# A decoder layer on one core: the last sums of squares and the scaled output rows are reordered, and the output goes out in six stores

## The reference, cut to what matters

```python
def rms_norm(x, w):
    return x * rsqrt(mean(x * x, axis=-1) + EPS) * w

h = x + rms_norm(mixer(rms_norm(x, n_mix_pre)), n_mix_post)
f = square(relu(rms_norm(h, n_ffn_pre) @ w_up)) @ w_down      # 1024 -> 4096 -> 1024
y = h + rms_norm(f, n_ffn_post)
```

## Time and profile before

| | us |
|---|---|
| median of 3 runs | 1686.3 (1685.75 to 1686.75) |
| profiled execution, its own time | 1687.35 |
| its span, first to last instruction | 1685.5 |
| PE busy | 1568.3 (93%) |
| DVE busy | 929.4 (55%) |
| ACT busy | 508.1 (30%) |
| POOL busy | 714.7 (42%) |
| last instruction of PE's 30 units ends | 1655.1 |
| last DVE instruction ends | 1677.7 |

### The profile page before, as it was taken

How to read it: one execution, slowest core, us unless ns; L and a number is a source line. 1 busy time by engine, 2 the same in 40 slices (tenths; PEclk the granted TensorE clock), 3 DMA queues, 4 the chain that set the end, 5 groups by cost and what they waited for, 6 DMA issues and landing times.

```text
span 1685.5 us, 27881 instructions
## 1 busy us (share of the span) xinstructions
PE 1568.3 (93%) x10984; PEld 1543.1 (92%) x10984; DVE 929.4 (55%) x1186; ACT 508.1 (30%) x693; POOL 714.7 (42%) x512
## 2 busy tenths in 40 slices
PE   5999999999999998999998969999998899999893
PEld 4999999899999997999998869999998899999893
DVE  5898969354473335011425936545556656565756
ACT  4100000322321224000223726544456142423332
POOL 3334434242244123344464634444444444545454
PEclk9999999999999999999999889999999999999997
DMA  5211121123221331111331053444447533324342
GB/s 168 88 49 46 44 64 44 32 76 100 75 94 44 95 103 34 50 44 46 103 109 32 26 198 123 138 149 155 156 140 252 194 126 123 123 92 141 102 137 109
DMA packets 83528, 169.47 MB, mean 101 GB/s; under 512 B 7392, under 2 KB 19424, under 8 KB 81136
## 3 DMA queue, kind: packets, MB, share of 16 engines
q1 hardware_dynamic: 69504, 144.61, 26.1%
q10 hardware_dynamic: 13936, 23.60, 4.3%
HBM read 124.82 MB, written 43.36 MB: 100 GB/s over the span
## 4 chain that ended last, share of the span: by engine, by line
PE 84%; DVE 8%; issue 2%; ACT 2%; DMA 2%; POOL 2%; SPq 0%; ACTq 0%; DVEq 0%; POOLq 0%
PE ps L610 42%; PE ps L952 31%; PE ps L868 3%; DVE tx_l L1845 2%; PE ps L881 2%; DVE fx_l L1845 1%; PE ps L791 1%; PE ps L710 1%; DVE xn_l L1556 1%; PE ps L709 1%; DVE fac L1956 1%; PE ps L636 1%; PE ps L713 1%; POOL w_l L524 1%; PE ps L724 1%
## 5 line engine op out<-in xcount | busy, mean ns | idle before, releaser
L521 POOL TENSOR_TENSOR w_h<-raw,zero 128x512 fp32r<-128x512 f32 x134 | 155.8, 1163 | 540.0 <-PE ps L610 411.6
L952 PE MATMUL ps<-tx_h,w_h 128*128 128x258 f32 x960 | 274.1, 286 | 18.7 <-DVE fac L1954 6.1
L952 PE MATMUL ps<-tx_l,w_h 128*128 128x258 f32 x960 | 273.2, 285 | 0.0
L952 PE MATMUL ps<-tx_h,w_l 128*128 128x258 f32 x960 | 273.2, 285 | 0.0
L579 POOL TENSOR_TENSOR w_l<-raw,w_h 128x512 fp32r<-128x512 f32 x120 | 181.9, 1516 | 183.8 <-ACT w_h L1333 183.7
L610 PE MATMUL ps<-xn_h,w_h 128*128 128x344 f32 x1128 | 248.4, 326 | 5.0 <-DVE xn_l L1556 4.0
L610 PE MATMUL ps<-xn_l,w_h 128*128 128x344 f32 x1128 | 242.0, 321 | 0.0
L610 PE MATMUL ps<-xn_h,w_l 128*128 128x344 f32 x1128 | 241.2, 320 | 0.0
L952 PE MATMUL ps<-fx_h,w_h 128*128 128x258 f32 x720 | 209.3, 291 | 28.7 <-DVE fac L2002 15.1
L952 PE MATMUL ps<-fx_l,w_h 128*128 128x258 f32 x720 | 207.1, 288 | 0.0
L952 PE MATMUL ps<-fx_h,w_l 128*128 128x258 f32 x720 | 207.0, 288 | 0.0
(11 more groups left out here) (269 smaller groups left out, 2629.4 us busy)
## 6 DMA issues: line engine op xcount, KB each, us to landing
raw<-wseq_dram SPq DMA_DIRECT2D x264, 256.0 KB, 2.7
hq_g<-hidden_scratch SPq DMA_DIRECT2D x14, 1032.0 KB, 8.1
hidden_scratch<-hq_g SPq DMA_DIRECT2D x8, 1032.0 KB, 5.9
stg_a<-hidden_scratch SPq DMA_DIRECT2D x7, 1032.0 KB, 6.7
stg_b<-hidden_scratch SPq DMA_DIRECT2D x7, 1032.0 KB, 6.4
hidden_scratch<-stg_b SPq DMA_DIRECT2D x6, 1032.0 KB, 5.8
rope<-rope_dram ACTq DMA_DIRECT2D x2, 2064.0 KB, 8.1
h_res<-xT_dram ACTq DMA_DIRECT2D x1, 4128.0 KB, 14.1
```

The costliest lines, as they stand in the source:

```text
L521: pool.tensor_tensor(hi, raw[:, s, :], zero[:, 0:1].broadcast_to([P, SLOT]), ALU.add).then_inc(w_hi, 1)
L952: out = pe.matmul(ps[:, 2 * n + s, 0:HC], RINGS[q % RING][wa][:, kk * P:(kk + 1) * P], OPS[x][xb][:, QK * kh + kk, at_:at_ + HC], start=(i ...
```

## The change

The squares: DVE's folds are written by a helper `fold(squares, row, shift, n)`. In the last unit all seven rows 0 to 6 of t = 0 are folded into row 0 by the end of step 3, in five folds instead of two; PE takes the first half's sum ahead of step 6, as ones on row 0 and ones on row 3 (8 PE instructions where 4 stood, in front of the step instead of in its middle). ACT runs `f_rms(0, 3)` directly behind the square of row 7 of t = 1, ahead of `down_gain(7, HALVES[1])`, e7 and the square of row 6.

The output rows: `out_norm` writes one scaled row into a PSUM pair (3, a or c) instead of into `fac`, and `out_residual` adds the residual from there into `fac`, one row per instruction. The rows of both halves are interleaved, so that an addition mostly follows its product by one other instruction. The addition e7 and `root_argument(1, b)` stand among the rows of the first half.

The stores: rows 0 to 2, 3 and 4, and 5 to 7 of each half leave as three stores; for t = 1 the one of rows 3 and 4 is last.

```diff
--- before.py
+++ after.py
@@ -493,12 +493,18 @@
 sp.dma_start(stg_a[:, 0:QK, 0:HT], hscr[:, KHALVES[0], HALVES[1]]).then_inc(h_ld[1], 16)
 sp.dma_start(stg_b[:, 0:QK, 0:HT], hscr[:, KHALVES[1], HALVES[1]]).then_inc(h_ld[1], 16)
 for t in range(2):
-    sp.wait_ge(y_dve, t + 1)
-    sp.dma_start(yT[:, 0:YD, HALVES[t]], fac[:, 0:YD, HALVES[t]]).then_inc(y_st, 16)
+    sp.wait_ge(y_dve, YD * t + 3)
+    sp.dma_start(yT[:, 0:3, HALVES[t]], fac[:, 0:3, HALVES[t]]).then_inc(y_st, 16)
+    if t == 0:
+        sp.wait_ge(y_dve, YD)
+        sp.dma_start(yT[:, 3:YD, HALVES[t]], fac[:, 3:YD, HALVES[t]]).then_inc(y_st, 16)
     sp.wait_ge(y_pool, t + 1)
     sp.dma_start(yT[:, YD:8, HALVES[t]], fac[:, YD:8, HALVES[t]]).then_inc(y_st, 16)
-
-sp.wait_ge(y_st, 16 * 4)
+    if t == 1:
+        sp.wait_ge(y_dve, 2 * YD)
+        sp.dma_start(yT[:, 3:YD, HALVES[t]], fac[:, 3:YD, HALVES[t]]).then_inc(y_st, 16)
+
+sp.wait_ge(y_st, 16 * 6)
 sp.wait_ge(cv_out, 16 * 2)
 sp.wait_ge(rp_st, 16 * PAIRS)
 for s in range(2):
@@ -932,7 +938,7 @@
     elif i == 6:
         evicted(pe, v, "e6b" if s else "e6a")

-def product(v, i, between=None):
+def product(v, i):

     q = STEPS * v + i
     a, b, c = BANKS[v]
@@ -954,8 +960,6 @@
                                 start=(i < 3 and kk == 0 and m == 0), stop=(kk == QK - 1 and m == 2),
                                 skip_group_check=True)
         out.then_inc(pm, 1)
-        if between and s == 0:
-            between()

 def h_stat(t):

@@ -975,15 +979,15 @@
                         start=first, stop=last)
     return out

-def f_stat_first():
-
-    pe.wait_ge(f_ad, 6)
-    pe.wait_ge(h_cp, 2)
-    f_ones(0, True, True, 3).then_inc(f_st, 1)
-
 for v in range(NV):
     for i in range(STEPS):
-        product(v, i, f_stat_first if (v, i) == (NV - 1, STEPS - 1) else None)
+        if (v, i) == (NV - 1, STEPS - 1):
+            pe.wait_ge(f_ad, 7)
+            pe.wait_ge(h_cp, 2)
+            f_ones(0, True, False, 3)
+            pe.wait_ge(f_sq, 8)
+            f_ones(3, False, True, 3).then_inc(f_st, 1)
+        product(v, i)
         if v == 3 and i in (0, 3):
             h_stat(i // 3)
 pe.wait_ge(f_ad, 8)
@@ -1503,14 +1507,14 @@
 down_gain(5, slice(0, T))
 down_gain(6, HALVES[0])
 down_gain(7, HALVES[0])
-act.wait_ge(f_ad, 4)
+act.wait_ge(f_ad, 5)
 evicted(act, v, "e6b")
 down_square(6, 7, 8, 1)
+f_rms(0, 3)
 down_gain(7, HALVES[1])
 evicted(act, v, "e7")
 down_square(7, 6, 7, 1)
 down_gain(6, HALVES[1])
-f_rms(0, 3)
 f_rms(1, BANKS[v][1])


@@ -1970,27 +1974,27 @@
     if p == 0:
         staged_lo(STEPS * g + 4)
     if v == NV - 1:
-        dve.wait_ge(f_sq, 5)
-        dve.tensor_tensor(hq_g[:, 0:2, :], hq_g[:, 0:2, :], hq_g[:, 2:4, :], ALU.add).then_inc(f_ad, 1)
+        fold(5, 0, 2, 2)
+        fold(5, 0, 1, 1)
     add(m2, 1, c, step_done(v, 2), True)
     if p == 0:
         staged_lo(STEPS * g + 5)
     if p == 3 and g + 1 < GROUPS:
         staged_lo(STEPS * (g + 1))
     if v == NV - 2:
-        dve.wait_ge(f_sq, 2)
-        dve.tensor_tensor(hq_g[:, 0:2, :], hq_g[:, 0:2, :], hq_g[:, 2:4, :], ALU.add).then_inc(f_ad, 1)
+        fold(2, 0, 2, 2)
     if v == NV - 1:
-        dve.wait_ge(f_sq, 6)
-        dve.tensor_tensor(hq_g[:, 4:6, :], hq_g[:, 4:6, :], hq_g[:, 6:8, :], ALU.add).then_inc(f_ad, 1)
+        fold(6, 4, 2, 2)
     add(m2, 0, a, step_done(v, 3), True)
     if p == 0:
         staged_lo(STEPS * g + 6)
     if p == 3 and g + 1 < GROUPS:
         staged_lo(STEPS * (g + 1) + 1)
     if v == NV - 2:
-        dve.wait_ge(f_sq, 4)
-        dve.tensor_tensor(hq_g[:, 4:6, :], hq_g[:, 4:6, :], hq_g[:, 6:8, :], ALU.add).then_inc(f_ad, 1)
+        fold(4, 4, 2, 2)
+    if v == NV - 1:
+        fold(6, 4, 1, 1)
+        fold(7, 0, 2, 1)
     evicted(dve, v, "e4")
     add(m2, 0, c, step_done(v, 4))
     if p == 3 and g + 1 < GROUPS:
@@ -2000,21 +2004,19 @@
         dve.wait_ge(pm, step_done(v, 5) - 1 + s)
         f = two(fac[:, m2, HALVES[1]])[:, s, :]
         dve.tensor_tensor(f, ps[:, 2 * a + s, 0:HC], f, ALU.add).then_inc(ev_d, 1)
-        if v == NV - 1 and s == 0:
-            dve.wait_ge(f_sq, 8)
-            dve.wait_ge(f_ad, 4)
-            dve.tensor_tensor(hq_g[:, 0:2, :], hq_g[:, 0:2, :], hq_g[:, 2:4, :], ALU.add
-                              ).then_inc(f_ad, 1)
-            dve.wait_ge(f_ad, 5)
-            dve.tensor_tensor(hq_g[:, 0, :], hq_g[:, 0, :], hq_g[:, 1, :], ALU.add).then_inc(f_ad, 1)
     if v + 1 < NV:
         first_sums(v + 1)
-    else:
-        dve.tensor_tensor(hq_g[:, 4, :], hq_g[:, 4, :], hq_g[:, 5, :], ALU.add).then_inc(f_ad, 1)
-        dve.wait_ge(f_ad, 7)
-        dve.wait_ge(f_sq, 9)
-        dve.tensor_tensor(hq_g[:, 4, :], hq_g[:, 4, :], hq_g[:, 6, :], ALU.add).then_inc(f_ad, 1)
-    add(m1, 1, a, step_done(v, 6), True)
+        add(m1, 1, a, step_done(v, 6), True)
+
+folds = [0]
+
+def fold(squares, row, shift, n):
+
+    dve.wait_ge(f_sq, squares)
+    dve.wait_ge(f_ad, folds[0])
+    dve.tensor_tensor(hq_g[:, row:row + n, :], hq_g[:, row:row + n, :],
+                      hq_g[:, row + shift:row + shift + n, :], ALU.add).then_inc(f_ad, 1)
+    folds[0] += 1

 def root_argument(t, n):

@@ -2023,23 +2025,23 @@
     dve.scalar_tensor_tensor(pair(n), pair(n), 1.0 / D_MODEL, two(hms[:, HALVES[t]]),
                              ALU.mult, ALU.add).then_inc(f_den, 1)

-def out_norm(t, n):
+reads = {}
+
+def out_norm(t, m, n, dst):

     dve.wait_ge(f_rp, t + 1)
-    for m in range(YD):
-        f = two(fac[:, m, HALVES[t]])
-        out = dve.scalar_tensor_tensor(f, f, vec[:, V_FPOST + m:V_FPOST + m + 1], pair(n),
-                                       ALU.mult, ALU.mult)
-    out.then_inc(y_n, 1)
-
-def out_residual(t):
-
-    dve.wait_ge(y_n, t + 1)
+    if dst in reads:
+        dve.wait_ge(y_dve, reads[dst])
+    dve.scalar_tensor_tensor(pair(dst), two(fac[:, m, HALVES[t]]), vec[:, V_FPOST + m:V_FPOST + m + 1],
+                             pair(n), ALU.mult, ALU.mult).then_inc(y_n, 1)
+
+def out_residual(t, m, src):
+
+    dve.wait_ge(y_n, YD * t + m + 1)
     dve.wait_ge(h_ld[t], 32)
-    f = fac[:, 0:QK, HALVES[t]]
-    dve.tensor_tensor(f, f, stg_a[:, 0:QK, HALVES[1 - t]], ALU.add)
-    f = fac[:, QK, HALVES[t]]
-    dve.tensor_tensor(f, f, stg_b[:, 0, HALVES[1 - t]], ALU.add).then_inc(y_dve, 1)
+    x = stg_a[:, m, HALVES[1 - t]] if m < QK else stg_b[:, m - QK, HALVES[1 - t]]
+    dve.tensor_tensor(two(fac[:, m, HALVES[t]]), pair(src), two(x), ALU.add).then_inc(y_dve, 1)
+    reads[src] = YD * t + m + 1

 for v in range(UPV):
     if v == 0:
@@ -2048,12 +2050,35 @@
     up_unit(v)
 for v in range(UPV, NV):
     down_unit(v)
+v = NV - 1
+a, b, c = BANKS[v]
 root_argument(0, 3)
-out_norm(0, 3)
-root_argument(1, BANKS[NV - 1][1])
-out_residual(0)
-out_norm(1, BANKS[NV - 1][1])
-out_residual(1)
+fold(9, 4, 2, 1)
+out_norm(0, 0, 3, c)
+out_residual(0, 0, c)
+dve.wait_ge(pm, step_done(v, 6))
+f = two(fac[:, KT - 2, HALVES[1]])
+dve.tensor_tensor(f, pair(a), f, ALU.add).then_inc(ev_d, 1)
+out_norm(0, 1, 3, c)
+evicted(dve, v, "e7")
+out_norm(0, 2, 3, a)
+out_residual(0, 1, c)
+out_norm(0, 3, 3, c)
+out_residual(0, 2, a)
+root_argument(1, b)
+out_norm(0, 4, 3, a)
+out_residual(0, 3, c)
+out_residual(0, 4, a)
+out_norm(1, 0, b, 3)
+out_norm(1, 1, b, a)
+out_residual(1, 0, 3)
+out_norm(1, 2, b, c)
+out_residual(1, 1, a)
+out_norm(1, 3, b, 3)
+out_residual(1, 2, c)
+out_norm(1, 4, b, a)
+out_residual(1, 3, 3)
+out_residual(1, 4, a)


 def rope_tables():
```

## The result

| | before | changed |
|---|---|---|
| median of 6 runs (us) | 1686.26 (1684.97 to 1686.84) | 1677.91 (1675.77 to 1680.82) |
| ratio of the times | | 0.9946 (0.9934 to 0.9959) |
| span of the profiled execution | 1685.5 | 1673.8 |

The change saves 8.35 us by the medians and 9.1 us (7 to 11) by the ratio. The forecast was 1677.4, 8.9 us less. The two profiled executions differ by 11.7, more than the change explains: in the changed one the last unit's addition of step 1 is at 1637.05, where it was at 1640.00, and the work ahead of it is the same. **So from here on I count from this addition** and, behind it, from T, the end of the first half's roots on ACT (1658.87 before, 1653.52 changed).

What follows compares the result with a forecast made beforehand. PE bounds the kernel until late in the last unit, then DVE's rows, then the stores. Earlier root 2.6, root to DVE's end 4.4 and stores 1.9 make 8.9 us: 1686.3 becomes 1677.4, range 1675.8 to 1680.8.

Steps and rivals of the forecast that it cites:

- e7: DVE's late addition in the last unit, now among the first half's output rows; forecast to cost 0.6 us there.
- step 1: Last unit: the one-row fold waits for POOL, so PE waits about 0.5 us on DVE's addition; priced at 0.55.
- rival (a): Last unit: folds stop PE for longer, roots 1.3 to 2.6 us later, 1678.7 to 1680.0; chance 0.10.
- step 2: First half's roots on ACT end 2.6 us earlier, with the first scaled row near 1656.3.
- Rival (d): First half's roots are not earlier, held by ACT or a fold; 6.3 of 8.9 us left, 1680.0; chance 0.04.
- step 3: DVE's output rows: every residual row at 0.70 whatever POOL does, POOL's four instructions at 3.45 to 3.73.
- rival (c): Output rows: PSUM input does not lift the POOL-DVE lock; 1688.9 in full, 1681 to 1687 partly; chance 0.05.
- step 4: End of the rows: DVE's last row near 1670.7, POOL's end within 0.5 us of it.
- step 5: Output stores: bytes flow without a gap over the last three stores; gain 1.9 us.
- Rival (b): Last stores: a 0.9 us pause ahead of each of the last two, POOL instruction slower; 1679.2 to 1680; chance 0.07.

Runs made afterwards that it cites:

- run 6: Changed kernel with the one-row fold (5, 0, 1, 1) moved behind the addition that followed it: median 1675.85, ratio 0.9946 to the kernel before.
- run 3: Kernel before with only the changed kernel's folds, ones and early roots, rows and stores as before: 1684.8 beside 1687.65, ratio 0.9986.
- run 1: Changed kernel with scaled rows kept in SBUF, so each residual adds two SBUF tiles: 1685.85 beside 1687.65 for the kernel before, ratio 0.9992.

## Why the prediction held, point by point

The steps came as forecast, most within 0.2 us. That the median came within 0.5 us of 1677.4 is luck in part: the six runs of the changed kernel lie between 1675.77 and 1680.82.

**The folds and PE's stand (step 1).** Right in place and cause: the one-row fold met POOL's low part, e3 came late, and PE waited. A size was off: I priced the delay at 0.55, and it cost 0.71 (run 6): 0.63 up to the first matmul behind the wait and 0.08 up to the second. The slack of e4 and of row 7's square held, so rival (a) did not happen.

**The earlier roots (step 2).** 2.6 forecast, 2.40 measured (18.87 to 16.47). The 0.2 is the larger stand and the ones: PE's first ones start at 1649.01 and `root_argument` at 1650.95, 1.94 later, where I had 1.9. What I did not see is that this term does not stand alone. The prediction followed the changed kernel's own order, in which e7 is third, and there the term holds; carried over to the old rows it gives only 1.35 (run 3). Rival (d), that only part of the root's gain arrives, did not happen in the changed kernel, but it has a real form: e7 behind the rows.

**The rows (step 3).** The term of the sum that carried most was right to 0.04 us: 14.44 against 14.4. A scaled row into PSUM, for which I had no row, takes 0.754 and the next follows at 0.66 (0.68 assumed); the residual takes 0.690. The same scaled row into SBUF takes 0.738 (median of ten, run 1). The lock of rival (c) is real for two inputs in SBUF, at 7.6 us (run 1), and is not there with one in PSUM. The Trainium skill's rule on the port (SBUF — State Buffer, "Who interferes with whom") says that whoever issues first blocks the other. In run 1 each long residual started inside an instruction of POOL's and ended 0.55 behind it, so the trace agrees.

The other rule of the Trainium skill weighed, that reading PSUM costs more than reading SBUF (VectorE: DVE Perf Modes, the section on the TRN2 errata), would have been 0.065 us per residual, an estimate from that page. Measured: 0.690 with one input in PSUM against 0.681 for the unhindered ones with both in SBUF (run 1), 0.009 us. The measurement decides: for these shapes ten residuals pay 0.1 us for PSUM, not 0.65.

**POOL (step 4).** 14.57 against 14.5, each of its instructions at 3.45 to 3.48. It ends 0.13 behind DVE, and its store is second of the last three.

**The stores (step 5).** 20.28 against 20.3, bytes without a gap, and 1.95 for the stores alone (1.9). Rival (b), a pause ahead of each store, did not happen; 11 stores ended where a queue without pauses ends them (18.82, expected 18.6 to 19.0), though between 1669.0 and 1670.0 of that trace the queue was busy for only 0.89 and 0.72 of the two halves, 0.2 us short. What the prediction had in its numbers and did not draw out: the last store's size matters less than when the queue starts.

The sum, 8.9, stands against 8.75 by the traces, 8.35 by the medians and 9.1 by the ratio.

## What to carry to other kernels

Where a DVE instruction with both inputs in SBUF meets a long one of POOL, one waits for the other, and the views used here name no wait: look for durations of the same shape that differ, and see whether one ends a fixed time behind the other. Passing the intermediate value through a free PSUM bank removes it, for 0.02 us per scaled row and 0.01 per residual (run 1 against the changed kernel). A gain ahead of a chain counts only if the next chain is fed as early, here by the one addition moved up; and where the last stores flow without a gap, their beginning has to be moved, not their end.

## What the runs showed of the hardware beyond that

The executions of one kernel scatter by 5 us here for the changed one (1675.77 to 1680.82) and by 9.5 for run 3 (1680.85 to 1690.35), and the traces put 2.95 of the 11.7 us between the two profiled spans ahead of the last unit. Stretches of 5 us near the start (after the stretch and its length, busy time of PE, PEld, DVE, ACT and POOL; third from the right the granted clock), of the kernel before:

```profile
25.00:30.00 5.00, 2.38 (x13) 2.02 (x13) 5.00 (x4) 0.65 (x1) 4.19 (x2) 0.93 0.20 52
30.00:35.00 5.00, 5.00 (x26) 5.00 (x25) 5.00 (x8) 3.91 (x8) 0.76 (x1) 0.73 0.00 0
```

and of the changed one:

```profile
25.00:30.00 5.00, 5.00 (x34) 4.91 (x33) 5.00 (x7) 3.00 (x6) 4.04 (x2) 1.00 0.18 52
30.00:35.00 5.00, 4.56 (x29) 4.12 (x28) 4.60 (x7) 1.72 (x4) 1.30 (x1) 1.00 0.00 0
```

In the first PE had stood for half of 25 to 30 us, and between 30 and 35 the clock was granted at 0.73 on average, between the upper level of 2.4 GHz and the lower of 1.2; in the second PE was busy throughout and kept the upper level. The same instructions run there in both, and the run with rows and stores alone shows the first picture too. At 40 us the changed kernel is 3.70 us ahead: ACT's L1000 of the kernel before starts at 40.35, the same instruction (L1004) at 36.65.

Later part of this is given back. The stretches from 540 us on, of the kernel before:

```profile
545.00:550.00 5.00, 3.76 (x25) 3.15 (x23) 0.00 (x0) 1.98 (x3) 2.32 (x2) 1.00 0.15 46
550.00:555.00 5.00, 2.64 (x20) 2.65 (x21) 1.22 (x6) 2.45 (x4) 0.00 (x0) 1.00 0.46 119
```

and of the changed one:

```profile
540.00:545.00 5.00, 3.83 (x26) 3.50 (x25) 0.00 (x0) 1.62 (x2) 2.32 (x2) 1.00 0.14 48
545.00:550.00 5.00, 2.73 (x16) 2.45 (x15) 0.00 (x0) 2.22 (x3) 0.00 (x0) 0.86 0.49 159
550.00:555.00 5.00, 5.00 (x31) 5.00 (x30) 2.17 (x8) 0.60 (x1) 0.57 (x1) 0.80 0.01 4
```

Here it is the changed kernel whose clock falls, to 0.86 and 0.80 on average. Ahead of that PE was busy for 3.83 and 2.73 us of two stretches; the kernel before has nearly the same stop (3.76 and 2.64) and keeps the upper level. Behind it ACT's L1152 of before is at 559.35 and its counterpart at 557.12: the lead is 2.23 us, and it grows to the 2.95 by the last unit. Why one execution takes the one way and another the other was not tried. A gain of 2 us at the end can be read here only from a point inside the trace, or from many runs.
